# Differential heads' values in column halves with a feature-major head norm, in a two-layer hybrid trunk kernel

## The reference

```python
def diff_attention(q, k, v, lam_p, norm_g, lam_init):      # 4 heads, values of 64, keys of 2 x 32
    a1 = attend(q[..., 0, :], k[..., 0, :], v, scale)      # softmax(q1 k1) v
    a2 = attend(q[..., 1, :], k[..., 1, :], v, scale)
    o = a1 - lam * a2
    o = rmsnorm(o, norm_g) * (1.0 - lam_init)              # per token and head, over the head's 64 values
...
up = jnp.einsum('btnw,nwd->btnd', br, lp['w_branch'])      # br: the four mixers' outputs, 256 wide each
merged = jnp.sum(jax.nn.sigmoid(mgate) * up, axis=2)
h = h + g1 * (merged @ lp['w_out'])
xm2 = rmsnorm(h, lp['norm2']) * (1.0 + sc2) + sh2
h = h + g2 * hier_moe(xm2, ...)    # top group, then 2 of its 4 experts; 16 experts of 1024 x 256
```

## Time and profile before

| | before |
|---|---|
| median of 3 runs | 2408.72 us (2404.51 to 2408.88) |
| profiled execution | 2407.84 us, span 2405.8 us |
| TensorE (PE) busy | 2225.7 us, 93% |
| VectorE (DVE) busy | 881.2 us, 37% |
| ScalarE (ACT) busy | 571.0 us, 24% |
| GpSimd (POOL) busy | 566.8 us, 24% |
| mean granted TensorE clock | 0.965 |

### The profile page before, as it was taken

How to read it: one execution, slowest core, us unless ns; L and a number is a source line. 1 busy time by engine, 2 the same in 40 slices (tenths; PEclk the granted TensorE clock), 3 DMA queues, 4 the chain that set the end, 5 groups by cost and what they waited for, 6 DMA issues and landing times. The chain is left out here.

```text
span 2405.8 us, 32467 instructions
## 1 busy us (share of the span) xinstructions
PE 2225.7 (93%) x12832; PEld 1343.7 (56%) x12832; DVE 881.2 (37%) x1737; ACT 571.0 (24%) x1168; POOL 566.8 (24%) x588
## 2 busy tenths in 40 slices
PE   5999999999999998899779999999999999969992
PEld 2555677776676654333245556777767766533330
DVE  1000555555554435111140008455645543431115
ACT  3100231113444411111140003211134443111112
POOL 0000202325000711555210002033330035045541
PEclk8999999999999998999979999999999999969996
DMA  9342212113111936988664312112121157069855
GB/s 353 132 152 71 61 57 67 55 42 117 39 52 54 326 131 247 366 314 341 216 238 155 119 30 86 57 57 68 57 88 46 35 209 269 35 269 382 313 173 183
DMA packets 188981, 364.57 MB, mean 152 GB/s; under 512 B 54480, under 2 KB 129936, under 8 KB 175136
## 3 DMA queue, kind: packets, MB, share of 16 engines
q1 hardware_dynamic: 135136, 201.44, 24.6%
q0 software_dynamic: 39168, 136.39, 14.9%
q10 hardware_dynamic: 14528, 24.69, 3.1%
HBM read 427.85 MB, written 54.10 MB: 200 GB/s over the span
## 5 line engine op out<-in xcount | busy, mean ns | idle before, releaser
L592 PE MATMUL psum<-arena,h 128*128 128x320 f32 x2048 | 620.5, 445 | 11.5 <-ACT h L610 8.6
L592 PEld LDWEIGHTS psum<-arena,h 128*128 128x128 f32 x2048 | 370.4, 191 | 154.6 <-issue 14.7
L419 PE MATMUL psum<-arena 128*128 128x413 f32 (+3 forms) x1184 | 391.5, 492 | 6.4 <-ACT arena L446 6.4
L419 PEld LDWEIGHTS psum<-arena 128*128 128x128 f32 x1184 | 211.1, 193 | 178.2 <-issue 171.0
L1946 PE MATMUL psum<-arena 128*64 128x512 f32 x1152 | 261.5, 608 | 10.3 <-DMA arena<-in_moe_w,wrow 7.2
L1689 POOL DMA_INDIRECT arena<-in_moe_w,wrow x144 | 143.1, 993 | 231.8 <-issue 136.6
L1946 PEld LDWEIGHTS psum<-arena 128*64 128x64 f32 x1152 | 83.3, 140 | 163.5 <-issue 160.3
L1839 PE MATMUL psum<-arena 128*128 128x320 f32 x512 | 138.9, 433 | 4.0 <-DVE arena L2091 2.0
L1850 PE MATMUL psum<-arena 128*128 128x512 f32 x320 | 140.5, 594 | 0.0
L473 DVE COPY arena<-psum 128x413 f32<-128x413 f32 (+2 forms) x36 | 17.6, 490 | 327.0 <-PE psum L419 325.8
L1969 PE MATMUL psum<-arena 128*64 128x512 f32 x576 | 131.5, 598 | 0.9 <-ACT arena L2044 0.9
(11 more groups left out here) (326 smaller groups left out, 2749.2 us busy)
## 6 DMA issues: line engine op xcount, KB each, us to landing
...
gate_rows<-h SPq DMA_DIRECT2D x128, 160.0 KB, 1.8
arena<-gate_rows SPq DMA_DIRECT2D x16, 1280.0 KB, 11.4
...
```

The costliest lines, as they stand in the source:

```text
L419: ins = nc.tensor.matmul(psum[:, 4 + i % 4, 0:w], lhs, rhs, start=(k == 0), stop=(k == KD - 1))
L592: ins = nc.tensor.matmul(psum[:, gate_bank(i), 0:HT], gw[c % 2][:, k, f:f + P], gate_xt[:, k, half:half + HT], start=(k == 0), stop=(k == ...
```

## The change

In attention, the differential heads go the GQA heads' way. Two heads of a tile are closed together: the values of each are 64 columns of weights, the turned probabilities stream, and the output is feature-major in `o2_ps`. `combine` divides by the first sum in a second pass. VectorE copies the pair's output, squares it into `squares`, and TensorE multiplies the squares by `by_head`, a block diagonal of ones, two items after the pair began its second head; so each row holds its head's sum of squares for each token. VectorE copies these sums into `vn` (`take_sums`, ahead of `combine`). ScalarE takes the square root of all of `vn` (128x1280) after the item `DIFF_DONE + 2`; after its last item VectorE takes the reciprocal of `vn` and multiplies it and the gain column `dcol` into `o_all`.

In the merge, four blocks per tile are turned instead of six, and VectorE copies two parts into `oT`. In the last layer, SP loads the first two weight parts of expert 0 into stream 0 ahead of the routing, and GpSimd's loads for unit 0 come after `gather(0)`, with row numbers out of bounds if that unit's expert is expert 0. Between experts and next layer, `fuse` is cut in two, `mix` and `add_in`, with the scaling of the tile before between them, and ScalarE's deviation of tile t comes ahead of its copies of tile t - 1.

```diff
+by_head, squares, dcol = ar(QPRE + 1364, P), ar(QPRE + 1492, P), ar(QPRE + 1620, 1)
...
-o_ps = psum[:, 5, P:P + DK]
 o2_ps = psum[:, 5, 2 * P:3 * P]
-closes = [j < H or n % 2 == 1 for n, (t, j) in enumerate(att_items)]
-outs_of = lambda n: sum(closes[:n])
+head_ps = psum[:, 5, 3 * P:4 * P]
+sums_at = [i + 2 for i, (t, j) in enumerate(att_items) if j in (1, 3)]
+outs_of = lambda n: n // 2
...
-        for dst, src in ((qg, a["gqa_qnorm"]), (kg, a["gqa_knorm"]), (dng, a["diff_norm"]), (sgn, a["sgu_norm"]),
+        for dst, src in ((qg, a["gqa_qnorm"]), (kg, a["gqa_knorm"]), (sgn, a["sgu_norm"]),
                          (gng, a["gdn_norm"])):
             sp.dma_start(dst, src[ds(l, 1)].rearrange("a d -> (a d)").partition_broadcast(P)).then_inc(B["in_b"], 16)
+        for half in range(2):
+            sp.dma_start(dcol[half * DK:(half + 1) * DK, :], a["diff_norm"][ds(l, 1)].rearrange("a d -> d a"),
+                         allow_slow_non_contiguous=True).then_inc(B["in_b"], 16)
...
             if i:
                 pe.wait_ge(B["pt_done"], i)
                 pe.wait_ge(B["o_done"], outs_of(i))
+            if i in sums_at:
+                pe.wait_ge(B["head_in"], sums_at.index(i) + 1)
...
                 if j < H:
-                    val = (vcb if t and k == 0 else ptok[:, k, C_VB:C_VB + 256])[:, j * DK:(j + 1) * DK]
-                    ins = nc.tensor.matmul(o_ps, PT[i % 2][:, k, :], val, start=start, stop=stop)
+                    val = (vcb if t and k == 0 else ptok[:, k, C_VB:C_VB + 256])[:, (j - 1) * DK:(j + 1) * DK]
                 else:
                     val = vcd if t and k == 0 else ptok[:, k, C_VD:C_VD + 128]
-                    for kv in range(2):
-                        rows = slice(kv * DK, (kv + 1) * DK)
-                        ins = nc.tensor.matmul(o2_ps[rows, :], val[:, rows], PT[(i - 1 + kv) % 2][:, k, :],
-                                               start=start, stop=stop)
+                for first in range(2):
+                    rows = slice(first * DK, (first + 1) * DK)
+                    ins = nc.tensor.matmul(o2_ps[rows, :], val[:, rows], PT[(i - 1 + first) % 2][:, k, :],
+                                           start=start, stop=stop)
             ins.then_inc(B["o_ps"], 1)
+        def head_sums(n):
+            pe.wait_ge(B["sqr"], n + 1)
+            pe.wait_ge(B["pt_done"], sums_at[n])
+            nc.tensor.matmul(head_ps, by_head, squares, start=True, stop=True).then_inc(B["head_ps"], 1)
...
-            if i and closes[i - 1]:
+            if i and i % 2 == 0:
                 values(i - 1)
+            if i in sums_at:
+                head_sums(sums_at.index(i))
...
-                act.wait_ge(B["o_ps"], outs_of(i - 1 if closes[i - 2] else i))
+                act.wait_ge(B["o_ps"], outs_of(i))
             own.send(nc.scalar.activation(PT[i % 2][:, 0:nk // P, :].rearrange("p a b -> p (a b)"),
                                           bank(4, 2)[:, 0:nk], ACT.Copy), B["pt_done"])
-            if i == DIFF_DONE + 1:
+            if i == DIFF_DONE + 2:
                 act.wait_ge(B["ssd"], 1)
-                own.tell(nc.scalar.activation(dss, dss, ACT.Sqrt, bias=eps_col, scale=1.0 / DK), B["sstd"])
+                own.tell(nc.scalar.activation(vn, vn, ACT.Sqrt, bias=eps_col, scale=1.0 / DK), B["sstd"])
...
-        own.link(vec.tensor_scalar(dng, dng, lamc[:, 1:2], None, ALU.mult))
+        own.link(vec.tensor_tensor(dcol, dcol, lamc[:, 1:2], ALU.mult))
+        own.link(vec.memset(by_head, 0.0))
+        for half in range(2):
+            rows = slice(half * DK, (half + 1) * DK)
+            own.link(vec.memset(by_head[rows, rows], 1.0))
...
-                own.send(vec.scalar_tensor_tensor(E_[:, 0, 0:nk], E_[:, 1, 0:nk], r[:, 2:3], E_[:, 0, 0:nk],
-                                                  ALU.mult, ALU.add), B["comb"])
+                own.link(vec.scalar_tensor_tensor(E_[:, 0, 0:nk], E_[:, 1, 0:nk], r[:, 2:3], E_[:, 0, 0:nk],
+                                                  ALU.mult, ALU.add))
             else:
                 own.tell(vec.reciprocal(r[:, 0:1], sums[:, 0:1]), B["rl"])
-                own.send(vec.tensor_scalar(E_[:, 0, 0:nk], E_[:, 0, 0:nk], r[:, 0:1], None, ALU.mult), B["comb"])
+            own.send(vec.tensor_scalar(E_[:, 0, 0:nk], E_[:, 0, 0:nk], r[:, 0:1], None, ALU.mult), B["comb"])
...
             t, j = att_items[i]
             v.wait_ge(B["o_ps"], outs_of(i + 1))
+            at = 256 + P * (j // 2) if j < H else 768 + P * HEADS[H::2].index(j - 2)
+            own.tell(vec.tensor_copy(o_all[:, t, at:at + P], o2_ps), B["o_done"])
             if j < H:
-                at = 256 + j * DK
-                own.send(vec.tensor_scalar(o_all[:, t, at:at + DK], o_ps, rl[:, i % 2, 0:1],
-                                           None, ALU.mult), B["o_done"])
-            else:
-                at = 768 + P * HEADS[H::2].index(j - 2)
-                own.send(vec.tensor_copy(o_all[:, t, at:at + P], o2_ps), B["o_done"])
+                n = sums_at.index(i + 2)
+                if n:
+                    v.wait_ge(B["head_ps"], n)
+                own.send(vec.tensor_tensor(squares, o_all[:, t, at:at + P], o_all[:, t, at:at + P], ALU.mult),
+                         B["sqr"])
+        def take_sums(n):
+            v.wait_ge(B["head_ps"], n + 1)
+            own.tell(vec.tensor_copy(vn[:, n // 2, (n % 2) * P:(n % 2 + 1) * P], head_ps), B["head_in"])

...
-        def square_b():
-            own.settle(B["o_done"])
-            own.link(vec.tensor_tensor(vn, o_all[:, :, 256:512], o_all[:, :, 256:512], ALU.mult))
-            own.tell(vec.tensor_reduce(dss, vn.rearrange("p t (h d) -> p (t h) d", h=H), AX.X, ALU.add), B["ssd"])
-
-        def normalize_b(t):
-            x = o_all[:, t, 256:512].rearrange("p (h d) -> p h d", h=H)
-            own.link(vec.tensor_tensor(x, x, bc(dss[:, t * H:(t + 1) * H], [H, DK], 2), ALU.mult))
-            own.link(vec.tensor_tensor(x, x, bc(dng, [H, DK], 1), ALU.mult))
-
         v.wait_ge(B["ostd"], 1)
         own.link(vec.reciprocal(oss, oss))
         maxima(0)
         for i in range(NI + 1):
             if i + 1 < NI:
                 maxima(i + 1)
+            if i in sums_at:
+                take_sums(sums_at.index(i))
             if i < NI:
                 combine(i)
-            if i and closes[i - 1]:
+            if i and i % 2 == 0:
                 outputs(i - 1)
             if i % 4 == 2 and 10 <= i < 10 + 4 * NT:
                 normalize_a((i - 10) // 4)
-            if i == DIFF_DONE:
-                square_b()
-            if i == DIFF_DONE + 2:
-                v.wait_ge(B["sstd"], 1)
-                own.link(vec.reciprocal(dss, dss))
-                normalize_b(0)
-                normalize_b(1)
-            if i == DIFF_DONE + 3:
-                for t in range(2, NT):
-                    normalize_b(t)
+            if i == sums_at[-1]:
+                own.tell(vec.memset(rl[:, 0, 3:4], 0.0), B["ssd"])
+        v.wait_ge(B["sstd"], 1)
+        own.link(vec.reciprocal(vn, vn))
+        own.link(vec.scalar_tensor_tensor(o_all[:, :, 256:512], o_all[:, :, 256:512], dcol, vn,
+                                          ALU.mult, ALU.mult))
...
+    at = HU if u == 0 and l + 1 == DEPTH else unit_of(u)
...
+    def load_first_expert():
+        sp.wait_ge(M["out_ps"], 2 * NT)
+        for i, name in enumerate(("moe_w1", "moe_w3")):
+            sp.dma_start(wup[0][:, i * 2048:(i + 1) * 2048].rearrange("p (k n) -> p k n", k=KD),
+                         a[name][ds(l, 1), 0, :, :].rearrange("a (p k) n -> p (a k) n", p=P))\
+              .then_inc(M["early"], 16)
...
         load_ada(4)
+    else:
+        load_first_expert()
...
         if t >= 2:
             pe.wait_ge(M["tr_done"], t - 1)
-        for k in range(KD - 2):
-            ins = nc.tensor.transpose(bank(2 * (t % 2), 2)[:, k * P:(k + 1) * P],
+        for n, k in enumerate((0, 1, 4, 5)):
+            ins = nc.tensor.transpose(psum[:, t % 2, n * P:(n + 1) * P],
                                       o_all[:, t, k * P:(k + 1) * P], ident)
         ins.then_inc(M["tr_ps"], 1)
...
-            if n == H - 1:
-                pe.wait_ge(M["gqa_in"], 1)
+            if n % 2 == 1:
+                pe.wait_ge(M["turned_in"], n // 2 + 1)
...
+        own.tell(nc.scalar.activation(oT.rearrange("p (b k) t -> p b k t", b=H)[:, 0::2, :, t * P:(t + 1) * P],
+                                      psum[:, t % 2, :].rearrange("p (b k t) -> p b k t", b=2, k=2), ACT.Copy),
+                 M["tr_done"])
...
+    if last:
+        for t in range(NT):
+            std_of(t)
             if t + 2 < NT:
                 weigh(t + 2)
-        else:
-            if t >= 1 and t + 1 < NT:
+    else:
+        std_of(0)
+        weigh(2)
+        copy_turned(act, own, X, 0)
+        std_of(1)
+        for t in range(2, NT):
+            std_of(t)
+            if t + 1 < NT:
                 weigh(t + 1)
```

(54 more changed lines are left out.)

24 lines of the change are left out of this document (8 added, 16 removed).

## The result

The changed kernel takes 2433.82 us (median of 4 runs, 2432.84 to 2435.14), the kernel before 2406.63 in its 4 runs (2404.51 to 2408.88) on the same chip. The ratio is 1.0108, with a 95% interval of 1.0096 to 1.0121: slower by 1.1%, where the forecast was 2433.5. The profiled execution took 2434.09 around a span of 2431.9, 26.1 more than the span before.

A forecast was written before the change was run, and what follows sets the result against it. TensorE, busy 93%, bounds nearly everywhere, but in attention items a VectorE–TensorE ring is already as long. Terms 12.5 + 0.9 + 13.0 + 2.0 - 2.4 - 0.4 = +25.6 on 2407.8 give 2433.4, predicted as 2433.5 us, range 2416 to 2443.

The forecast's parts named there:

- Items of 640 keys, +12.5: Attention loop, four tiles in each layer: VectorE's added pass makes each tile 1.56 us longer, +12.5 us over eight tiles.
- +1.1, +0.1, +0.15 and +0.25: Per tile of 640 keys, us: first three items together, then the fourth, fifth and sixth item, together +1.56.
- the ring: Attention items: scores, maxima, combine, turn and next scores form a loop, already as long as TensorE's work; 5.80 or 5.53 after.
- The bound of -14: Attention items of 640 keys: lower limit, -14 us, if all of TensorE's saving came through.
- the rival that TensorE keeps the pace (2407): Attention items: VectorE's 0.55 us pass finds slack, -14 stands for +12.5, 2407 us, not slower; chance 0.07.
- End of attention, +13.0: Behind the last item: reciprocal of 128x1280, 8.2 us, and a multiplication delay the merge by 6.5 us per layer.
- Both rivals about its price: Reciprocal at attention's end: cheap as a pass, 1.4 ns a column, 2419, chance 0.08; or a quarter dearer, 2438, 0.05.
- TensorE's clock at the merge, +2: Merge start: idle TensorE resumes at the 1.2 GHz level, 0 to 3 us a layer, taken as 1.
- Hand-over, -2.4: From experts to next layer, once: two of VectorE's three waits ahead of tile 2's turn go; -2.4 us (0 to -3.4).
- Early weights, -0.4: Last layer's experts: early loads of expert 0 bring hardly anything, second expert product gets weights hardly earlier; -0.4 us.
- The rival of 5 us: Last layer's experts: the early weights bring all of their 2 MB, -5 us, total 2429; chance 0.10.
- Start of attention, +0.9: Attention's start: one more `diff_norm` transfer issued ahead of `sgu_b`, for which VectorE waits; +0.9 us both layers (0 to 2).

The follow-up runs named there:

- the shifted filling: Kernel before with TensorE's gate filling shared out otherwise, five steps in a differential item and three in a grouped-query item instead of four each: 2412.79 us, ratio 1.0017.
- the roots last: Changed kernel with each tile's sums inverted at once, the square root taken last and the multiplication ahead of the last output copy: 2421.17 us, ratio 1.0054.

## Why the prediction was right, step by step

**Items of 640 keys, +12.5 foreseen.** Right in mechanism, and nearly in size. A tile got 1.6 longer, as foreseen (37.8 to 39.4). The prediction's parts, +1.1, +0.1, +0.15 and +0.25, were measured as +1.24, -0.02, +0.11 and +0.23 (its 4.83 for odd items is a slip, since 5.10 - 0.29 - 0.12 + 0.06 is 4.75; it moves a tile by under 0.1). Leaving out the pass returned all of it, and one more of the kind cost 2.1 a tile. Two things were missing. The tile of 128 keys, put at 0, brought 0.6 us a layer. And 1.26 a layer came from one item in which TensorE's clock fell, which nothing in the kernel before shows. What is left of the 7.8 is 6.0 a layer, against 6.2 foreseen.

**A step that was wrong, though the sum held.** I read that VectorE already released the turn at 1872.67, because it followed 0.12 behind the copy, and the row itself shows no wait for VectorE. More filling on the kernel before lengthened that very item: there TensorE's work set the pace, with VectorE just ahead. The turn at 1867.46, with 0.51 of idle, was truly VectorE's, but it is the turn of a grouped-query head, whose pass the change doesn't add. The two chains were within some tenths of each other. So the pass didn't lengthen a ring that was already the bound; it made the ring the bound, and TensorE's 2.1 us a tile, removed at the same time, became waiting. Both readings give nearly the same sum here, but not in other edits: it is why I expected the shifted filling to gain 7 us on the kernel before, where it lost.

**The bound of -14, and the rival that TensorE keeps the pace (2407).** Not even without the pass does TensorE's saving come through: 1.3 us a layer against 7. The bound counted TensorE's work and not the ring under it.

**End of attention, +13.0.** 14.8: 13.5 from the last copy to the merge, and 1.3 from ScalarE's root and its table ahead of the last copies of P, for which 0.8 was in the sum. The reciprocal took 8154 ns, where 8.2 us were foreseen: from 644 to 1280 columns it is 6.25 ns for each further column, and 6.27 had been carried over; the multiplication 1.55 in place of 1.7. Both rivals about its price fall: it is neither as cheap as a pass nor dearer on long rows. The Trainium skill, "VectorE: DVE Perf Modes", section "First, the fixed hardware budget", from which 8.3 ns a column had been estimated, is borne out in that a division is several times a pass, and not in its size. That the tail hung on this instruction was shown by leaving it out (6.5 less in each layer), and that it hung on its place and not on the work by the roots last, which moved the multiplication too: tails of 4.0 again.

**TensorE's clock at the merge, +2.** The clock fell as foreseen, to 0.50, and cost next to nothing: the merge of the last layer was 0.1 longer. The other profiles agree. From the merge's first copy to the cast of the row numbers the last layer took 172.9 to 174.8 us in the six kernels that began there at 0.50, and 173.1 to 176.6 in the eight that began at 1.00. In the kernel without the reciprocal the clock was still 1.00 there, and TensorE soon ran out of work, with the branches' weights and gates still on their way; that the transfers hide the cold clock fits this, but I did not test it by itself.

**Hand-over, -2.4.** -3.3 between the landmarks of the table and -4.0 counted from the last expert product, the same alone on the kernel before. Tile 2's turn came 2.3 earlier, counted from the last expert product, as the term had it; it left out that the two tiles behind it gain 1.6 more, and that tile 2's turn no longer runs at the low clock.

**Early weights, -0.4.** +1.7 in this profile, and +1.5 to +2.3 to the fourth product, chip by chip, so this term had the wrong sign. The early load did act: GpSimd's queue moved 134.3 MB in place of 136.4, so the rival of a change that doesn't act falls. The reason against the 5 us was the right one, GpSimd's issues that move nothing: unit 2's load was issued 13.2 behind the cast of the row numbers, as forecast, where it had been 11.9. What I had not priced is that this lateness, 1.3 us, costs more than the 2 MB win. The rival of 5 us names a gain that is there, but only in another order, and smaller: 1.7 to 2.6 us against the kernel before, 3.0 to 4.4 against the changed kernel's order.

**Start of attention, +0.9.** -1.7, of which -1.8 is layer 0, so the sign was wrong there. VectorE waits for `sgu_b` in both kernels, first before the change, then after it:

```profile
556.81 0.56 DVE L1479 TENSOR_TENSOR arena<-arena,small 128x384 f32<-128x384 f32 x1 [4.03 <-DMA small<-in_sgu_b]
...
554.88 0.56 DVE L1491 TENSOR_TENSOR arena<-arena,small 128x384 f32<-128x384 f32 x1 [2.16 <-DMA small<-in_sgu_b]
```

This is no scatter: the wait is 3.65 to 4.03 in the three kernels with the old transfers and 2.06 to 2.53 in the eleven with the new ones, although there is one transfer more. Why they land sooner was not tested. (The kernel with only the hand-over changed reached the first turn 1.5 earlier too, but it was that much ahead before attention began, and waited 4.03.) In the last layer VectorE waited 2.36 against 0.75:

```profile
1742.83 0.56 DVE L1491 TENSOR_TENSOR arena<-arena,small 128x384 f32<-128x384 f32 x1 [2.36 <-DMA small<-in_sgu_b]
```

but the first turn came only 0.2 later than the work ahead of it.

**Where luck helped.** The sum came within 0.5 us of the 26.1 measured, closer than its terms. The loops of attention came out 3.1 above their term, the ends of attention 1.8 and the early weights 2.1. The start of attention (2.6 below), the merges with their clock (3.1) and the hand-over (0.9) went the other way.
